# A two-layer attention-and-experts kernel on one core: the rotary product gets its own counter, score tiles are normalised in pairs, and low halves of weights wait behind them

## What is computed

```python
h = modulate(rms_norm(x, g_mix[l]), sh1, sc1)          # and hc for the context tokens
... = split_in(h @ w_in[l])
o_b = neighbourhood_attention(na_q, na_k, na_v, kc_na, vc_na, na_rpb[l])
o_c = window_attention(apply_rope(sw_q, cos, sin), apply_rope(sw_k, cos, sin), sw_v, kc_sw, vc_sw, sw_sink[l])
x = x + gt1 * merge_branches((o_a, o_b, o_c), (ga, gb, gc), w_branch[l], w_out[l])
if not last:   # layer 0 alone
    co_b = context_attention(cna_q, kc_na, vc_na, None)
    co_c = context_attention(csw_q, kc_sw, vc_sw, sw_sink[l])
x = x + gt2 * expert_choice_ffn(...)                    # 16 experts
```

## Time and profile before

| | |
|---|---|
| three runs | 1887.91 us median (1886.74 to 1888.42) |
| profiled execution | 1892.0 us, of which the traced span is 1890.1 us |
| PE matmul busy | 1702.9 us, 90% of the span |
| DVE, ACT busy | 779.1 us (41%), 477.5 us (25%) |
| granted PE clock, mean | 0.965 of full speed |
| attentions and branches of layer 0 | about 155 to 470 us of the span |
| the same of layer 1 | about 1150 to 1400 us |
| experts of layer 1 | about 1480 us to the end |

### The profile page before, as it was taken

How to read it: one execution, slowest core, us unless ns; L and a number is a source line. 1 busy time by engine, 2 the same in 40 slices (tenths; PEclk the granted TensorE clock), 3 DMA queues, 4 the chain that set the end, 5 groups by cost and what they waited for, 6 DMA issues and landing times.

```text
span 1890.1 us, 26478 instructions
## 1 busy us (share of the span) xinstructions
PE 1702.9 (90%) x10846; PEld 984.4 (52%) x10846; DVE 779.1 (41%) x1751; ACT 477.5 (25%) x1047; POOL 113.2 (6%) x149
## 2 busy tenths in 40 slices
PE   4999989999999899999998699989998997777865
PEld 2887767667765333333332398877783332222222
DVE  3365545666443233333332474567653221211112
ACT  3224444454223000000000344455441000000001
POOL 1001210000001000000000101200001000000000
PEclk8999999999998999999999899999999999999988
DMA  9432322115777899999999864337779999999996
GB/s 343 152 89 68 104 65 68 48 34 182 276 277 302 365 428 428 427 428 428 428 427 428 320 201 123 97 117 235 240 299 389 426 427 426 426 427 426 427 427 282
DMA packets 149874, 543.82 MB, mean 288 GB/s; under 512 B 9786, under 2 KB 92032, under 8 KB 124156
## 3 DMA queue, kind: packets, MB, share of 16 engines
q1 hardware_dynamic: 147356, 535.98, 72.2%
q0 software_dynamic: 2400, 6.16, 1.2%
HBM read 539.13 MB, written 2.98 MB: 287 GB/s over the span
## 4 chain that ended last, share of the span: by engine, by line
PE 65%; DMA 24%; DVE 6%; ACT 3%; issue 1%; SPq 0%; POOL 0%; DVEq 0%; ACTq 0%
PE bank L2030 19%; PE bank L1893 11%; PE bank L1894 10%; PE bank L1895 10%; DMA ring<-in_w_exp_down 7%; DMA ring<-in_w_exp_gate 6%; DMA ring<-in_w_exp_up 4%; PE bank L1808 2%; DMA split_slot<-in_w_exp_gate 2%; DMA split_slot<-in_w_exp_down 2%; PE bank L1943 2%; PE bank L2004 2%; PE bank L1920 2%; PE bank L1930 2%; DVE WL L1488 2%
## 5 line engine op out<-in xcount | busy, mean ns | idle before, releaser
L2030 PE MATMUL bank<-ring,XEP 128*32 128x256 f32 (+1 forms) x2576 | 409.1, 620 | 32.4 <-DMA ring<-in_w_exp_up 18.1
L1893 PE MATMUL bank<-HH,WH 128*128 128x512 f32 (+1 forms) x864 | 312.7, 362 | 6.6 <-ACT GT L1320 4.6
L1894 PE MATMUL bank<-HL,WH 128*128 128x512 f32 (+1 forms) x864 | 302.2, 350 | 0.0
L1895 PE MATMUL bank<-HH,WL 128*128 128x512 f32 (+1 forms) x864 | 301.5, 349 | 0.0
L2030 PEld LDWEIGHTS bank<-ring,XEP 128*32 128x32 f32 (+1 forms) x2576 | 121.4, 130 | 289.6 <-issue 238.4
L1488 DVE TENSOR_TENSOR WL<-ring,WH 128x1024 fp32r<-128x1024 f32 (+1 forms) x172 | 186.1, 1083 | 177.0 <-ACT WH L1267 176.6
L1740 DVE TENSOR_TENSOR X<-X,bank 128x512 f32<-128x512 f32 x192 | 119.0, 683 | 193.8 <-PE bank L2049 100.8
L2030 PE MATMUL bank<-ring,HIDT 128*32 128x256 f32 (+1 forms) x1264 | 157.4, 487 | 45.2 <-DMA ring<-in_w_exp_down 45.2
L1893 PEld LDWEIGHTS bank<-HH,WH 128*128 128x128 f32 x864 | 165.8, 192 | 54.7 <-issue 25.4
L1267 ACT CAST WH<-ring 128x1024 fp32r<-128x1024 f32 (+1 forms) x172 | 158.0, 927 | 99.1 <-PE bank L1895 65.2
L1895 PEld LDWEIGHTS bank<-HH,WL 128*128 128x128 f32 x864 | 165.7, 192 | 21.2
(11 more groups left out here) (223 smaller groups left out, 1935.4 us busy)
## 6 DMA issues: line engine op xcount, KB each, us to landing
ring<-in_w_exp_gate SPq DMA_DIRECT2D x57, 2048.0 KB, 30.4
ring<-in_w_exp_up SPq DMA_DIRECT2D x53, 2048.0 KB, 32.1
ring<-in_w_exp_down SPq DMA_DIRECT2D x51, 2048.0 KB, 37.7
ring<-in_w_ada SPq DMA_DIRECT2D x48, 1024.0 KB, 7.5
ring<-in_w_in SPq DMA_DIRECT2D x40, 1024.0 KB, 5.9
split_slot<-in_w_exp_up SPq DMA_DIRECT2D x8, 2048.0 KB, 28.9
split_slot<-in_w_exp_down SPq DMA_DIRECT2D x8, 2048.0 KB, 31.4
ring<-in_w_in SPq DMA_DIRECT2D x28, 512.0 KB, 5.2
```

The lines of the kernel that those rows point to most:

```text
L1893: mm(t, wh, hi[:, k, 0:b.n], start=k == 0, stop=False)
L1894: mm(t, wh, lo[:, k, 0:b.n], start=False, stop=False)
L1895: last = mm(t, wl, hi[:, k, 0:b.n], start=False, stop=k == b.kk - 1)
L2030: last = mm(out_bank[tw * g:tw * g + tw, 0:nw], stationary(k), w[:, g::G] if spread else w[:, nw * g:nw * g + nw], start=k == 0, stop=k == ...
```

## The change

Four edits. (1) The rotary product no longer takes a number of `blk_ready`; it has a semaphore of its own, `rot_ready`. (2) It is no longer put off to the next flush but issued three k steps after its block, or at the next `attention` or `sk`/`sq` end, whichever is first (`turn_due`). (3) Both units of a pair are normalised at the same place: k step 2 in `sw` of layer 0, half of the fill elsewhere; `na` of layer 1 keeps its old places. WL steps are held until then in `na` of layer 0 and `sw` of layer 1 too. (4) `na` of layer 0 now also gives 30% of its k steps to a latent and 20% to a context pair. Also, `values` of a short `sw` fill in layer 0 comes at k step 2, where it was 3.

```diff
-    def tile(self, act=False, dve=False, bank=None):
+    def tile(self, act=False, dve=False, bank=None, counted=True):
         n = self.tiles
-        self.tiles += 1
+        self.tiles += counted
...
         if b.out in ("sk", "sq"):
+            turn_due(9)
             finish_low()
...
             def rope():
-                b.rot_tile = P.tile(dve=True)
+                b.rot_tile = P.tile(dve=True, counted=False)
...
-            P.deferred.append(rope)
+            P.rope_due.append([3, rope])
+
+    def turn_due(steps):
+
+        while P.rope_due and P.rope_due[0][0] <= steps:
+            P.rope_due.pop(0)[1]()
+        for due in P.rope_due:
+            due[0] -= 1
...
             P.add("k", blk=atom[1], k=atom[2])
+            turn_due(1)
...
-            early = br == "sw" and not last
             fill = list(fill)
+            turn_due(9)
             finish_low()
             for n_pair, pair in enumerate(pairs):
                 P.add("score", pair=pair)
                 per = -(-nk_atoms // len(pairs))
-                if early:
+                if not last:
                     long = round(nk_atoms * 0.3)
                     per = long if n_pair % 2 == 0 else nk_atoms // 2 - long
-                    at_ = {2: lambda: (P.flush(), normalise(pair[0]), normalise(pair[1])), 3: values, -(-per * 7 // 10): lower}
-                else:
-                    at_ = {-(-per * 3 // 10): values, -(-per * 9 // 20): (lambda: normalise(pair[0])), -(-per * 7 // 10): (lambda: (normalise(pair[1]), lower()))}
+                both = 2 if br == "sw" and not last else -(-per // 2)
+                at_ = [(both, lambda: normalise(pair[0])), (both, lambda: normalise(pair[1]))]
+                if br == "na" and last:
+                    at_ = [(-(-per * 9 // 20), lambda: normalise(pair[0])), (-(-per * 7 // 10), lambda: normalise(pair[1]))]
+                at_ = sorted(at_ + [(-(-per * 3 // 10), values), (-(-per * 7 // 10), lower)], key=lambda a: a[0])
...
-            if s.kind == "score" and l == 0 and s.pair[0].br == "sw":
+            if s.kind == "score" and (l == 0 or s.pair[0].br == "sw"):
                 scored = 2
...
-                            dve.wait_ge(blk_ready, b.rot_tile.ready)
+                            dve.wait_ge(rot_ready, b.rope)
...
-                            mm(t[:, 0:SEQ], ROT, QT[:, 0:SEQ], start=True, stop=True).then_inc(blk_ready, 1)
+                            mm(t[:, 0:SEQ], ROT, QT[:, 0:SEQ], start=True, stop=True).then_inc(rot_ready, 1)
```

More of the change, by code:

```diff
@@ L213, in __init__ @@
         self.turned, self.lower, self.turned_low = [], [], []
+        self.rope_due = []
     def add(self, kind, **kw):
@@ L535, in attention @@
                         n += 1
-                        if n in at_:
-                            at_.pop(n)()
+                        while at_ and at_[0][0] <= n:
+                            at_.pop(0)[1]()
                 while fill and fill[0][0] != "k":
                     emit(fill.pop(0))
-                for rest in at_.values():
+                for _, rest in at_:
                     rest()
@@ L940, in hybrid_dit_kernel @@
         qk_hi = sem("qk_hi")
+        rot_ready = sem("rot_ready")
         qk_ready = sem("qk_ready")
```

## The result

The changed kernel took 1865.1 us, the median of four runs (1863.13 to 1866.02), against 1888.2 for the kernel before on the same occasion (four runs, 1886.7 to 1894.0). The ratio is 0.9868, 95% interval 0.9852 to 0.9884. With the runs of the later experiments there are 8 of the changed kernel (median 1865.1, 1860.4 to 1866.0) and 51 of the one before (median 1888.9, 1885.6 to 1899.3). The gain is 23 to 24 us; the forecast was 1859.0, range 1855 to 1868.

A forecast was written before the change was run, and what follows sets the result against it. PE was taken to bound layer 0's attentions, expert weight loads layer 1's experts. Terms 4.9 + 7.9 + 7.0 + 6.8 + 2.3 = 28.9 us took the profiled 1892.0 to 1863.1, the median 1887.9 to 1859.0; range 1855 to 1868.

The forecast's parts named there:

- Parts 1 and 3: Layer 0's attentions: six short PE waits for scaling go, 4.9 us; three longer latent-pair waits go, 7.0 us.
- Part 3: Layer 0's latent pairs, mainly `na` head pairs 2 and 3: longer fills and half-way scalings remove three waits, 7.0 us.
- Part 2: Layer 0's `sw`: rotary product with its own counter, a k step earlier, removes three long waits, 7.9 us.
- The slack that I counted from the earlier place: Layer 0's `sw`: with the product a k step earlier, the first tile is scaled 1.3 us before the turn.
- Part 4: Layer 0's attentions: three stretches partly at 1.2 GHz, each begun by a long wait, come back whole, 6.8 us.
- Part 5: Layer 1's attentions: a 2.15 us wait goes, three `sw` turns shorten, a new `na` wait costs; net 2.3 us.
- The new wait: Layer 1, `na` head pair 3: rotation ahead of the second scaling makes PE wait 0.9 us, net cost 0.6.
- the GT wait: Layer 1, around the `sk` rotation: PE's largest wait there, 4.63 us for ACT's GT, stays.
- the likeliest case: Whole kernel: the forecast's own case, 1855 to 1863 us, chance 0.68.
- The clock rival: Dense part: waits go but as much low clock turns up elsewhere, 6.8 us, so 1866 us; chance 0.13.
- The other rivals: Layer 0's context turns wait, 1867 (0.12); expert stream takes gain back, 1886 to 1888 (0.03); held low halves slow it (0.03).

The follow-up runs named there:

- before_again: The kernel before, run again with no edit for its spread and a second profile; median 1888.68 us, profiled execution 1889.1 us.
- after_again: The changed kernel, run again with no edit for its spread and a second profile; median 1863.04 us.
- hold_only: Kernel before, with only the holding of low weight halves until both scalings extended to `na` of layer 0 and `sw` of layer 1; 1871.80 us.
- even_fills: Changed kernel, with a quarter of the k steps for each pair in `na` of layer 0 instead of 30 and 20 per cent; 1864.59 us.
- counter_only: Kernel before, with only the rotary product counted by itself, at its old place in the order; 1881.61 us.
- no_hold: Changed kernel, with low weight halves held in `sw` of layer 0 alone, as before the change; 1867.69 us.
- pairs_only: Kernel before, with the changed kernel's fills and holds, rotary product untouched; 1881.17 us, eight runs in two heaps (1871.0 to 1872.3, 1879.4 to 1884.0).

## Why the prediction was right, and where its size was off

**Stage by stage.** Two profiles of each kernel, cut at three marks: the first expert load of layer 0, the first gather product (L2004, now L2017), the first issue of layer 1's expert stream.

| us | before | before_again | after | after_again |
|---|---|---|---|---|
| start to first expert load, layer 0 | 539.0 | 536.9 | 513.7 | 513.0 |
| to first gather product | 76.5 | 74.8 | 77.6 | 77.4 |
| to expert stream, layer 1 | 772.0 | 773.6 | 770.2 | 770.6 |
| to the end | 502.6 | 501.8 | 502.6 | 502.3 |

**Parts 1 and 3 (4.9 + 7.0 us).** The size was right, the cause given for Part 3 only in part. hold_only reached the first expert load at 523.8 us, 13.2 us earlier than before_again (both with some 6.8 us of low clock in the attentions); 1.3 of these lie ahead of the first scores (150.24 for 151.49), where the two kernels do the same, and 11.9 are left. The sum has 11.9. The step that failed is "latent pairs, which now get 14 or 10 k steps for 12 or 8", with the counter as a part of the cause: even_fills took the longer fills away and nothing returned, counter_only changed the counter and the wait of 3.8 us stayed. Low halves in front of the scaling made all nine waits of `na`, since holding them and nothing else removes all nine; the longest was the one whose WH stood behind dup. The hold does it alone (18.0 us with all that follows from it). Without it the other edits nearly do it too (no_hold lacks 2.6 us), most likely by the common place at half of the fill; that was not run by itself. Such worths don't add up.

**Part 2 (7.9 us).** Right: 7.5 us between the medians. The profile of counter_only reached the expert load 9.6 us earlier than before_again, 9.0 of them behind the first scores (150.89 for 151.49), with 3.4 us less low clock: 7.9 + 1.7 = 9.6 was to be expected there. The span is only 6.1 us shorter (1881.0 for 1887.1), mostly because the stretch behind the expert load took 77.6 us for 74.8, of which more below. The slack that I counted from the earlier place was not needed.

**The two halves nearly add up.** hold_only is 18.0 us below its kernel before, counter_only 7.5; 25.5 together, where the changed kernel is 24 below.

**Part 4 (6.8 us) was mis-sized, the largest error.** The mechanism holds: of the fourteen profiles (these twelve, before and after) the eight without a wait over 1 us in layer 0's attentions have no low stretch there, and in the six others each low stretch begins within 3 us of the end of a wait of 1.86 us or more. But not each wait is followed by one. In hold_only, windows around the three waits of 1.96 us:

```profile
310.00:325.00 15.00, 12.82 (x53) 0.89 0.22 72
345.00:360.00 15.00, 12.82 (x63) 1.00 0.34 105
380.00:395.00 15.00, 12.82 (x55) 0.89 0.34 107
```

Equal waits, and the second lost nothing. The profiled execution of before had 13.6 us of low clock here, which at half of it cost 6.8; before_again had 6.8, which cost 3.4 (the stretch was 2.9 us shorter). My sum took 6.8 from the profiled execution, which was right for that one, and then carried it whole to a median 4.1 us lower, that is to executions that had most likely not paid all of it: before_again's profiled execution, at 1889.1 close to the median of all runs, had paid 3.4. Some 3.4 us of the forecast are counted twice in this way. The Trainium skill (TensorE: Matmul & The Clock Gate, "What's actually happening") says that the same kernel shows a different number of cold matmuls at its start from run to run. The two profiles of the kernel before show the like in the middle of a kernel (13.6 and 6.8 us in the same stage), and that belonged in the sum, not only in a rival.

**A term that was missing.** Between the first expert load of layer 0 and the first gather product the changed kernel is 1.1 to 2.8 us longer. Windows of 70 us near the end of that stretch, of before, then before_again, then after:

```profile
545.00:615.00 70.00, 64.17 (x347) 0.93 0.75 294
```

```profile
545.00:615.00 70.00, 62.94 (x352) 0.98 0.75 296
```

```profile
520.00:590.00 70.00, 65.21 (x346) 0.90 0.75 294
```

That is 9.8, 2.8 and 14 us of low clock. It lies at the end of the stretch, in the routing behind the output projection: in the profile of after, PEclk is 1.00 up to 575 us of the span and 0.50 right behind that. PE's waits ahead of it are 0.78 us (at 574.10) and 0.68 us (at 575.43). So what held in the attentions, no low clock without a wait of 1.86 us or more, does not hold in the whole kernel. Over all fourteen profiles the length goes with the low clock in the stretch: 74.5 to 74.8 us with some 3 us of it (four profiles), 76.5 to 76.9 with 10 (three), 77.4 to 77.7 with 14 (seven). Of the eight profiles without long waits six are in the last group. What decides the group is open; nothing was tried on it.

**Part 5 (2.3 us).** From the gather product to the expert stream of layer 1 it is 1.8 us less in one pair of profiles and 3.0 in the other. The new wait was 0.84 for 0.9, the GT wait stayed at 4.63, the one of 2.15 went. That last one goes with the hold alone (hold_only) and without the hold too (no_hold). What the new wait costs can't be told apart here: hold_only, which has not got it, takes 300.0 us from layer 1's first block product to the expert stream; the changed kernel takes 301.5 and 300.9, but even_fills, with the same wait, 299.6.

**Together.** The time is 6.1 us above the forecast. Between the first two profiles it is 26.0 us for 28.9: 1.3 of the missing 2.9 lie ahead of the first expert load, 1.1 in the later low clock, 0.5 in layer 1. The other 3.2 come from the step to the median: the kernel before has it 4.1 us below its profiled execution, the changed kernel only 0.9, about the 3.4 us of clock counted twice. The second pair, 23.8 us between the spans where 25.5 was due without these 3.4, is short by 1.7. The time lay in the range 1855 to 1868, but above the likeliest case's own 1855 to 1863. The clock rival had the number, 1866, but only a small part of the cause: layer 0's attentions have no low clock left, and what turned up elsewhere is 3.4 to 10 us more of it in the routing behind layer 0's output projection, worth 1.1 to 2.6 us and not 6.8. That the other miss brought the time to its number is luck. The other rivals fell: PE waits at no context turn of layer 0, the expert stream moved by the full 25.98 us, and the held low halves brought no wait that a profile shows.

**Open.** The upper heap of pairs_only (8 to 12 us above the lower) and the runs of the kernel before at 1896 to 1899 us have no profile. All of them were taken in the first group of experiments; no run of the other two groups is more than 4 us above its median. The mean granted clock is lower in them, 0.963 to 0.969 against 0.970 to 0.973 in pairs_only; at which place, no trace here shows.

## What to carry to other kernels

Read what stands in front of the late instruction in its engine's queue, and what that one waits for in turn: here one weight conversion tied DVE's scaling to ACT's slowest copies, and one condition untied it. Test the edits of a bundle both ways, alone and left out, since two of them may do the same work and a third none. A clock loss seen in one profiled execution need not be in the median one (13.6 and 6.8 us of low clock here, in two executions of one kernel); profile the kernel before twice before it goes into a sum.

## What the hardware showed unexpectedly

Three equal idle gaps of 1.96 us on PE, some 35 us apart in a stretch that is otherwise full, were followed by about 3.4 us at 1.2 GHz after one or two of the three, and after different ones from execution to execution (five profiles, 7 of 15 gaps). The gap of 3.8 us was followed by low clock in all three profiles that have it, for about 6.8 us once and 3.4 twice. In the routing stretch of layer 0 the same clock fell behind waits of only 0.78 and 0.68 us, and in two executions of the kernel before it stayed low there for some 10 and some 3 us.
